# Both layers' MLP in seven products per pair, the second layer's modulation by TensorE pieces and inside its projection, and the weight sums spread over all stages

## The reference

```
h = rms_norm(x, norm1_g) * (1 + sc1) + sh1
proj = h @ w_in                                  # 24 tiles of 128 outputs
...   (DeltaNet with 4 heads, two attention groups)
x = x + g1 * (concat(o_a, o_b, o_c) @ w_out)     # 8 tiles
h2 = rms_norm(x, norm2_g) * (1 + sc2) + sh2
x = x + g2 * (square(relu(h2 @ w_ff1)) @ w_ff2)  # 1024 -> 4096 -> 1024
```

## Time and profile before

| | |
|---|---|
| median of 3 runs | 1834.06 us |
| the profiled execution's own time | 1830.43 us |
| its span, first to last instruction | 1828.6 us |
| PE busy | 1744.6 us (95%) |
| DVE busy | 1279.6 us (70%) |
| ACT busy | 841.4 us (46%) |
| POOL busy | 525.3 us (29%) |
| granted TensorE clock, mean | 0.983 of full |
| bytes moved by DMA | 316.66 MB |

### The profile page before, as it was taken

One profiled execution on the slowest core, in us unless ns is written; L12 is line 12 of the kernel. 1 busy time (PEld: TensorE's weight loads), 2 busy tenths in 40 slices (PEclk: granted clock), 3 DMA queues, 4 the chain that ended last, 5 costly groups with the idle time before them and its releaser, 6 DMA issues.

```text
span 1828.6 us, 33566 instructions
## 1 busy us (share of the span) xinstructions
PE 1744.6 (95%) x13554; PEld 1658.8 (91%) x13554; DVE 1279.6 (70%) x2127; ACT 841.4 (46%) x1459; POOL 525.3 (29%) x424
## 2 busy tenths in 40 slices
PE   5999999898999999999999999897989999999997
PEld 2889986798999999999999999676889999999997
DVE  2688675688635676776665567667887777788885
ACT  1555337633242231312326543574336656666663
POOL 5000001085442140421451000204742233233235
PEclk9999999999999999999999999998999999999998
DMA  8653223022567779687527861502432777886662
GB/s 345 251 207 90 77 78 62 3 63 88 187 217 231 287 221 342 231 274 285 167 98 194 187 150 52 111 1 76 101 113 86 226 231 244 300 286 246 223 208 85
DMA packets 128037, 316.66 MB, mean 173 GB/s; under 512 B 37828, under 2 KB 64236, under 8 KB 108172
## 3 DMA queue, kind: packets, MB, share of 16 engines
q1 hardware_dynamic: 121740, 279.49, 43.7%
q0 software_dynamic: 4608, 33.56, 9.5%
q10 hardware_dynamic: 1536, 1.48, 0.2%
HBM read 286.01 MB, written 95.49 MB: 209 GB/s over the span
## 4 chain that ended last, share of the span: by engine, by line
PE 79%; DVE 10%; DMA 4%; issue 3%; ACT 2%; SPq 1%; POOL 0%; POOLq 0%; DVEq 0%; ACTq 0%
PE PS L2287 47%; PE PS L2356 17%; DMA ADA<-ada 2%; PE PS L2561 1%; PE PS L2649 1%; PE PS L2723 1%; PE PS L2610 1%; PE PS L2589 1%; PE PS L2578 1%; DVE WHL L1543 1%; PE PS L2751 1%; DVE MPR L1749 1%; PE PS L2424 1%; DVE DT L1991 1%; PE PS L2598 1%
## 5 line engine op out<-in xcount | busy, mean ns | idle before, releaser
L2287 PE MATMUL PS<-HH,HI 128*128 128x320 f32 (+1 forms) x1280 | 300.2, 316 | 4.7 <-DVE HL L1498 4.7
L2287 PE MATMUL PS<-HL,HI 128*128 128x320 f32 (+1 forms) x1280 | 295.6, 312 | 0.0
L2287 PE MATMUL PS<-HH,LO 128*128 128x320 f32 (+1 forms) x1280 | 293.8, 311 | 0.0
L951 ACT CAST HI<-RAW 128x2048 fp32r<-128x2048 f32 x64 | 121.8, 1904 | 275.2 <-PE PS L2287 248.3
L2287 PEld LDWEIGHTS PS<-HH,HI 128*128 128x128 f32 x1280 | 215.6, 191 | 5.3 <-issue 5.2
L2287 PEld LDWEIGHTS PS<-HL,HI 128*128 128x128 f32 x1280 | 219.6, 192 | 0.0
L2287 PEld LDWEIGHTS PS<-HH,LO 128*128 128x128 f32 x1280 | 217.4, 191 | 0.0
L2356 PE MATMUL PS<-FB,WHL 128*128 128x320 f32 x1344 | 199.5, 309 | 6.6 <-DVE TMP L1626 3.6
L2356 PEld LDWEIGHTS PS<-FB,WHL 128*128 128x128 f32 x1344 | 197.1, 188 | 8.8 <-DVE WHL L1543 6.8
L2356 PE MATMUL PS<-HB,WHL 128*128 128x322 f32 (+1 forms) x1344 | 201.5, 312 | 2.4 <-DVE TMP L1626 1.4
L2356 PEld LDWEIGHTS PS<-HB,WHL 128*128 128x128 f32 x1344 | 200.5, 190 | 3.1 <-issue 3.1
(11 more groups left out here) (347 smaller groups left out, 2911.5 us busy)
## 6 DMA issues: line engine op xcount, KB each, us to landing
RAW<-ws SPq DMA_DIRECT2D x64, 1024.0 KB, 5.3
wp<-ws SPq DMA_DIRECT2D x32, 1024.0 KB, 8.4
RAWB<-wp SPq DMA_DIRECT2D x128, 256.0 KB, 4.0
WM<-adt SPq DMA_DIRECT2D x48, 512.0 KB, 9.7
RAWB<-ws SPq DMA_DIRECT2D x96, 256.0 KB, 3.7
FS<-hb SPq DMA_DIRECT2D x28, 640.0 KB, 8.4
ADA<-ada SPq DMA_DIRECT2D x16, 1024.0 KB, 7.7
wp<-ws POOLq DMA_DIRECT2D x16, 1024.0 KB, 10.1
```

The costliest lines, as they stand in the source:

```text
L951: nc.scalar.copy(HI[g % 2][:, :], RAW[g % 2][:, :]).then_inc(hi_ready, 1)
L2287: last = pe.matmul(bank(2 * u + a)[:, 0:e], w[:, cols], m[:, a * HT:a * HT + e], start=(k == 0 and f), stop=(k == KT - 1 and e_))
```

## The change

`FAST` is gone: both layers' MLPs run `fast_mlp`. The first layer's MLP loses 64 tiles of 48 matmuls and gets 32 pairs of 7 products of 12. What was done for the second layer during the first layer's plain MLP moves or goes:

* the 48 `mod_tile`s on DVE go. The second layer's modulation is now made as the first layer's: 8 pieces on TensorE in the first layer's MLP (`ADAF`, `MODF`, pairs 2 to 10), 8 more and 16 `mod_tile`s in the second layer's projection;
* each layer now has its own 32 copies and 32 sums. A layer's copies are issued in its projection (12), in its middle (14), behind its output projection (2) and in its MLP (4); its sums in its projection (8), in its attention (6), in its output projection (3) and in its MLP (15). Before, only the second layer had sums: 16 of them lay in the first MLP, 12 in the second projection, and 4 inside the second layer's DeltaNet loop; all 32 copies lay in the first layer's output projection and MLP;
* the second layer's projection follows a `fast_mlp`. Its last residuals are done in the order in which the pairs end, so the projection takes the blocks in the order 0, 1, 2, 4, 5, 6, 3, 7 (`NORM_AT`);
* near the end of the middle, own_values comes ahead of the first output tile's half.

```diff
+TILES = PT_ + 8
+SEQ = TILES // 2
+CHUNKS = SEQ + 32
...
-FAST = (1,)
...
+NORM_AT = (tuple(range(KT)), (0, 1, 2, 4, 5, 6, 3, 7))
+COPIES = {**{s: (s - 4,) for s in range(4, 16)}}
+OUT_SUMS = {1: 14, 3: 15, 5: 16}
+FAST_SUMS = {p: 17 + n for n, p in enumerate((1, 2, 3, 5, 6, 7, 9, 10, 11, 13, 14, 15, 17, 18, 19))}
...
+                        if l + 1 < DEPTH and i == 2 and p < 8:
...
+                            if p >= 2:
+                                sp.wait_ge(S["ada_mm"], o["ada_mm"] + 8 + p - 1)
+                            sp.dma_start(ADAF[p % 2][:, :, :], t["ada"][l + 1, p]).then_inc(ada_in[p % 2], 16)
...
+                    refill(g0)
                     if l == 0:
-                        refill(0)
                         sp.wait_ge(pro_mm, 8)
                     else:
-                        refill(g0)
-                        sp.wait_ge(S["w_mm"], o["w_mm"])
-                        sp.wait_ge(S["w_ev"], o["w_ev"])
+                        b = fast_base(l - 1)
+                        sp.wait_ge(F["c11"], b["c11"] + PAIRS7)
+                        sp.wait_ge(F["xup"], b["xup"] + 3 * HALF)
                         sp.dma_start(t["xs"], X[:, :, :, :]).then_inc(x_st, 16)
...
-                    if l == 0:
-                        ada_load(0)
-                        ada_load(1)
+                    if l:
+                        sp.wait_ge(nss, 2 * l + 1)
+                    ada_load(0)
+                    ada_load(1)
...
-                        if l == 0 and s == 1:
-                            sp.wait_ge(nsq, 15)
-                            sp.wait_ge(S["h_lo"], KT)
+                        if s == 1:
+                            sp.wait_ge(nss, 2 * l + 1)
+                            sp.wait_ge(S["h_lo"], o["h_lo"] + KT)
+                            if l:
+                                sp.wait_ge(x_st, 16 * l)
                             sp.dma_start(CBX[:, :, :], t["crow"].partition_broadcast(P)).then_inc(vb_in, 16)
...
+                        for d in COPIES.get(s, ()):
+                            sum_copy(l, d)
...
+                        if p in FAST_SUMS:
+                            weight_sum(l, FAST_SUMS[p])
...
-                    if l in FAST:
-                        for d in range(16, 28):
-                            weight_sum(l, d)
+                    for d in range(8):
+                        weight_sum(l, d)
...
+                    for d in range(8, 14):
+                        weight_sum(l, d)
...
-                        if l in FAST and s < 4:
-                            weight_sum(l, 28 + s)
...
+                        if l + 1 < DEPTH and w == 7 * PAIRS7 - 4:
+                            split_lo(l * SEQ + SEQ)
+                        if l + 1 < DEPTH and w == 7 * PAIRS7 - 2:
+                            for k in range(3):
+                                norm_lo(2 * l + 2, k)
...
                     lower_left(PAIRS7 - 1)
                     gated(PAIRS7 - 1, 1, 0, "c21")
+                    if l + 1 < DEPTH:
+                        shift_lo(2 * l + 2)
+                        for k in NORM_AT[l + 1][3:]:
+                            norm_lo(2 * l + 2, k)
...
-                    def next_mod(c, part, e):
...
-                    if l in FAST:
-                        fast_mlp(l, residual)
-                        continue
...
+                    b = fast_base(q // 2 - 1)
+                    pe.wait_ge(nsq, squared(q + 1))
+                    column_sums(SQA, True, False)
+                    pe.wait_ge(F["lsq"], b["lsq"] + 2)
+                    column_sums(SQ7, False, False)
+                    pe.wait_ge(F["lsq"], b["lsq"] + 3)
+                    column_sums(SQX, False, True).then_inc(nss, 1)
...
+                        p, i = divmod(w, PRODUCTS)
+                        if l + 1 < DEPTH and i == 3 and 2 <= p <= 9:
+                            ada(o, 8 + p - 2, ADAF[p % 2])
+                        if l + 1 < DEPTH and i == 3 and 3 <= p <= 10:
+                            adt(o, 8 + p - 3, MODF)
```

More of the change, by code:

```diff
@@ L71 @@
 V_N = 104
-MOD_AT = {(0, 1): 0, (1, 0): 8, (1, 1): 16, (2, 0): 24, (2, 1): 32, (3, 0): 40}
 MT = 48
@@ L309, in build @@
         YF = place("YF", [P, KT, 2, HT], F32, f1)
+        ADAF = [place(f"ADAF{i}", [P, KT, AC], F32, f1 + 512 + i * 8192) for i in range(2)]
+        MODF = [place(f"MODF{i}", [P, AC], F32, f1 + 512 + 16384 + i * 1024) for i in range(2)]
         assert at[0] <= 229344, at[0]
@@ L415, in squared @@
         def squared(n):
-            return 15 * n - 2 * len([l for l in FAST if 2 * l + 1 < n])
-        sums_copied = slot_in
+            return sum(15 if q == 0 else 13 if q % 2 else 11 for q in range(n))
         def stage(n):
@@ L673, in _ @@
                         sp.dma_start(SS[d][:, :, :], t["s0"][l, d]).then_inc(S["s0_in"], 16)
+                    for d in range(12, 20):
+                        sum_copy(l, d)
                     sp.wait_ge(S["apv"], o["apv"] + PAIRS)
@@ L681, in _ @@
                         gates_in(i)
+                        for d in range(2):
+                            sum_copy(l, 20 + 2 * (i - 2) + d)
                     sp.wait_ge(S["u1"], o["u1"] + 4 * NB)
@@ L1468, in _ @@
-                    done(7)
+                    fast_mlp(l)
                 act.wait_ge(nss, 5)
@@ L1807, in _ @@
                             taps(j - 2)
-                        if l == 0 and 2 <= j <= 9:
-                            ada_row(j - 2)
+                        if 2 <= j <= 9:
+                            ada_row(o, j - 2, MODB)
                         if j == 4:
@@ L1904, in _ @@
                                                                in1=TCQ[:, n, :], op0=ALU.mult, op1=ALU.mult).then_inc(S["map_"], 1)
-                        if l == 0 and j in MOD_IN:
+                        if j in MOD_IN:
                             first = sum(MOD_IN[x] for x in MOD_IN if x < j)
-                            for n in range(first, first + MOD_IN[j]):
-                                mod_tile(n, 4 * KT + n, WMX[n % 3], CBX)
+                            for n in range(MF * l + first, MF * l + first + MOD_IN[j]):
+                                mod_tile(n, 4 * KT + n - MF * l, WMX[n % 3], CBX)
                         for k in range(*LEAF_STEPS.get(j, (0, 0))):
@@ L2259, in _ @@
+                    fast_mlp(l, residual)
                 dve.wait_ge(nrt, 5)
@@ L2268, in _, with wstat @@
             def _(pe):
-                def wstat(tile, g, mh, ml, n, lo, c, norm=None, tail=None, ks=range(KT)):
+                def wstat(tile, g, mh, ml, n, lo, c, norm=None, tail=None, ks=range(KT), order=NORM_AT[0]):
                     s, u = g % 2, tile % 2
@@ L2276, in wstat @@
                         pe.wait_ge(S["w_ev"], tile - 1)
-                    for k in ks:
-                        pe.wait_ge(lo, c + k + 1)
-                        if k == 5 and norm is not None:
+                    for x in ks:
+                        k = order[x]
+                        pe.wait_ge(lo, c + x + 1)
+                        if x == 5 and norm is not None:
                             norm_turn(norm)
@@ L2287, in wstat @@
                                 last = pe.matmul(bank(2 * u + a)[:, 0:e], w[:, cols], m[:, a * HT:a * HT + e],
-                                                 start=(k == 0 and f), stop=(k == KT - 1 and e_))
+                                                 start=(x == 0 and f), stop=(x == KT - 1 and e_))
                     if KT - 1 in ks:
                         last.then_inc(S["w_mm"], 1)
-                def norm_sums(q):
-                    pe.wait_ge(nsq, 15 * (q + 1))
-                    for b in range(NB):
-                        last = pe.matmul(bank(4)[:, b:b + 1], SQA[:, toks(b)], one, start=True, stop=True)
-                    last.then_inc(nss, 1)
                 def norm_turn(q, to=2):
@@ L2416, in _ @@
                             pe.wait_ge(S["crt"], o["crt"] + 2)
-                        if l == 0 and 2 <= j <= 9:
-                            adt(j - 2)
+                        if 2 <= j <= 9:
+                            adt(o, j - 2, MODB)
                         if 4 <= j <= 11:
```

410 lines of the change are left out of this document (145 added, 265 removed).

## The result

The changed kernel takes 1921.47 us (median of 4 runs, 1920.06 to 1932.79); the kernel before, on the same chip, 1833.3 (1828.98 to 1835.09). The ratio is 1.050, 95% interval [1.047, 1.052]. The profiled execution took 1921.61 us, its span is 1919.7. I had predicted 1836, range 1819 to 1851.

A forecast was written before the change was run, and what follows sets the result against it. TensorE's order of matmuls was taken to bound the kernel. Terms -29.4 + 6 + 28.0 - 7.0 + 5 = +2.6 us gave 1836 us against a median of 1834.06, no measurable change; range 1819 to 1851.

The forecast's parts named there:

- First MLP, -29.4: First layer's MLP: -41.2 us for the fast form, plus 11.8 for 8 pieces and turns on PE, so -29.4 us.
- A piece's weights are asked for two pairs ahead, 28 us: First MLP: loads of the modulation pieces' weights are requested 28 us ahead; no cost was put on them.
- Room for transfers, +5: Both MLPs: DMA demand beyond the time available costs 4 us in the first and 1 in the second.
- what is asked for ahead: Both MLPs: look-ahead set against 19 and 13 us too much transfer; weights 8 products, 14 us, hidden blocks less.
- slower, by transfers: Full queue in pairs 2 to 7 of both MLPs, `hb` landing over 9 us, PE waiting: 18 us lost, 1850; chance 0.17.
- Its chain (store, TT, SP, weights): Both MLPs: `hb` lands late, then POOL's TT, then SP's order, and PE waits for weights; 18 us in place of 5.
- Passage, +6: Between first MLP and second projection: PE waits for x, behind residuals and three norm_lo blocks, 6 us.
- Second projection, +28.0: Second projection: pieces, turns and DVE waits 17.4, column sums 2.3, clock falls 3.6, CBX 2.9 and 1.8: +28.0 us.
- the term of CBX: Second projection: CBX lands late, PE waits 4.3 us instead of 1.4 (+2.9), and its clock may fall again (+1.8).
- Middles, -7.0: Second layer's middle: with the sums out of its loop, it gets 7.0 us shorter.
- the changed order at the end: End of each middle: three short waits replaced by three others, 0 us.
- The rival of starving transfers: Both MLPs: sums issued beside a busy DVE cost POOL and DVE 0.87 us each, at most 26 us, 1862; chance 0.02.

The follow-up runs named there:

- experiment 2: The changed kernel without the 15 weight sums that POOL issues inside each MLP (30 left out in all): 1851.65 us, ratio 1.010.
- experiment 3: The changed kernel with each of the 15 sums inside each MLP adding only 256 of 2048 columns: 1854.74 us, ratio 1.012.
- experiment 5: The changed kernel with the modulation's loads asked for one pair later and the 15 sums inside each MLP left out: 1835.66 us, ratio 1.001.
- experiment 4: The changed kernel with a second buffer for TT in pairs 0 to 9 of each MLP: 1929.1 us, ratio 1.049.
- experiment 9: The changed kernel with later modulation loads, PE's old order, sums respread, two TT buffers, and ACT reaching CBX a tile later in the second projection: 1839.54 us, ratio 1.004.
- experiment 7: The kernel before, with the 4 weight sums of the second layer's DeltaNet loop issued in attention, ahead of the loop: 1826.99 us, ratio 0.9967.
- experiment 6: The changed kernel with PE's order at the end of the middle as it was before: 1915.14 us, ratio 1.045.
- the last kernel: Experiment 9's kernel with six sums in each MLP, 14 in the projection, and a group's second sum not waiting for its first: 1840.4 us, ratio 1.004.
- the kernel ahead of it: Experiment 9's kernel with six sums in each MLP and 14 in the projection, done one after another: 1852.07 us, ratio 1.011.

## Why the prediction was wrong, step by step

* **First MLP, -29.4.** The term itself was right: freed of both causes the MLP is 426.0 us, and 453.7 - 29.4 is 424.3. "A piece's weights are asked for two pairs ahead, 28 us" is the first step that failed. I had costed the piece's arrival, and not SP's wait ahead of its load, nor named what is queued behind that wait: the loads of the weights. It cost 15.5 us alone and 31 in the changed kernel (16 and 29 by the medians).
* **Room for transfers, +5.** The second step that failed, and the larger: 23.7 + 29.3 us (449.7 - 426.0 and 441.8 - 412.5), and the 15.6 shared with SP's waits. The demand was computed about right, somewhat too high: by my prices pairs 2 to 15 of the second MLP have 14 x 9.3 us, 11 sums of 5 and 3 copies of 3, 194 us in 174.4, so 20 too much; it measured 187.0 - 174.4 = 12.6, since a sum is 4.0 and not 5. I had worked it out for pairs 2 to 7 alone (19 and 13 us too much) and then let "what is asked for ahead" hide nearly all of it. Look-ahead of 14 us covers one burst. A deficit in pair after pair is paid in full once it is spent. And 16.7 of the second MLP's 29.3 us fell behind pair 15, where three more sums lie beside the loads of the hidden blocks; that part went with the sums too (experiments 2, 3 and 5).
* **The rival "slower, by transfers" (0.17)** had the right mechanism and its sign: PE waits in pairs 2 to 7, `hb` lands after 10.6 us, over my 9. Its price, 18 us, was about a fifth of the 86 us by which the two MLPs miss their terms without transfers (480.8 - 424.3 and 441.8 - 412.5). Its chain (store, TT, SP, weights) was refuted by experiment 4 for pairs 0 to 9; weights were long on the way themselves, 7.7 us against the kernel before's

```profile
RAWB<-wp SPq DMA_DIRECT2D x128, 256.0 KB, 4.0
```

* **Passage, +6.** 6.1. As computed.
* **Second projection, +28.0.** +27.1. CBX was late as forecast: PE waited for MODB 3.4 us at its second piece, ACT stood at CBX ahead of it. In experiment 9's kernels that wait of 5.9 us was worth 8.3 in the stage; I had 4.7 for the term, wait and clock together. Without it the stage there was 216.2, 17.9 over the kernel before's 198.3, where my other terms come to 23.3. So the term of CBX was too low and the rest too high, and that the total came out at 27.1 is in part luck. ACT's wait in the changed kernel's timeline:

```profile
1018.64 1.92 ACT L1192 ACTIVATE CBX<-CBX 128x2048 f32<-128x2048 f32 x1 [2.07 <-DMA CBX<-crow]
```

And PE's, eight us on:

```profile
1026.87 1.93 PE L464 MATMUL PS<-ADA,SC 128*32 128x256 f32 x16 [3.41 <-DVE MODB L1465]
```

* **Middles, -7.0.** Right for the loop: experiment 7's second stretch is 7.1 us shorter (5.2 by the medians), and no such event is in the changed kernel's loops. But the changed order at the end brought a wait of 3.6 us in each layer, for which I had 0 (experiment 6: 6 us in all).
* **The rival of starving transfers** (0.02) had 26 us by the count of issues. Small sums kept all 30 issues beside a busy DVE, and 67 of the 70 us were back. So the price lies in the bytes. It was drawn from the Trainium skill's page "SBUF — State Buffer", section "SBUF: two separate sides"; no run here bears it out, and 3 us is all that experiment 3 leaves for it and for the bytes that its small sums still move.

## What to carry to other kernels

Ahead of a wait that you add to a queue, write down who has to pass for it to end, by the count that the waiting engine itself runs on; six products of lead on one engine turned a wait that looked met into 13 us. Compare the transfers' demand with the time stage by stage, and take any steady excess at full price: look-ahead hides a burst, not a rate. When work is moved to where an engine is idle, its serial latency counts too: here one sum takes 7 to 15 us of POOL's waiting, and the last of 14 in a row was issued 20 us behind the projection's end.

## What the runs showed of the hardware

A share of 1.00 of the DMA engines need not stop PE. In the first MLP of the changed kernel, as windows, the busy share is 1.00 and PE runs without a wait at the full clock, and 120 us earlier it is 0.87 and PE does a third less and is granted 0.83:

```profile
565.80:595.90 30.10, 22.03 (x134) 20.80 (x135) 12.99 (x28) 9.50 (x17) 4.93 (x5) 0.83 0.87 263
...
686.00:716.00 30.00, 30.00 (x206) 30.00 (x205) 21.53 (x42) 18.56 (x36) 9.79 (x10) 1.00 1.00 291
```

The waits of 4 us had a slower clock behind them (0.67 over 573.7 to 581.4 us), so a late weight costs more than its wait. A sum of 1 MB takes an estimated 4.0 us of all 16 engines in this mix (experiment 3). Two of them at once, in the projections of the last kernel, kept POOL waiting for 13 to 20 us; one alone, in the kernel ahead of it, for 7 to 14. Over the six places where the two kernels differ, POOL waited 99 us in place of 119: two together cost less than two in a row at four of them, and more at the two where sums in a row took only 7 to 9 us each.
